# A down projection by seven block products instead of eight, on a tuned encoder layer

## The reference

```python
    up = rmsnorm(x, g_ffn) @ w_up
    a, b = up[..., :D_FF], up[..., D_FF:]
    a_ext = jnp.concatenate([conv_hist.astype(a.dtype), a], axis=1)
    conv = conv_b + sum(a_ext[:, j:j + T] * conv_w[j] for j in range(CONV_W))
    x = x + (jax.nn.silu(conv) * b) @ w_down
```

## Time and profile before

| what | value |
|---|---|
| median of 3 runs | 891.83 us (891.22 to 893.13) |
| span of the profiled execution, first to last instruction | 890.1 us |
| PE busy | 858.1 us (96%) |
| PEld busy | 825.5 us (93%) |
| DVE busy | 518.1 us (58%) |
| ACT busy | 369.1 us (41%) |
| POOL busy | 108.3 us (12%) |
| chain that ended last | PE 85%, DVE 7%, ACT 4%, DMA 2% |

### The profile page before, as it was taken

One profiled execution on the slowest core, in us unless ns is written; L12 is line 12 of the kernel. 1 busy time (PEld: TensorE's weight loads), 2 busy tenths in 40 slices (PEclk: granted clock), 3 DMA queues, 4 the chain that ended last, 5 costly groups with the idle time before them and its releaser, 6 DMA issues.

```text
span 890.1 us, 16120 instructions
## 1 busy us (share of the span) xinstructions
PE 858.1 (96%) x6155; PEld 825.5 (93%) x6155; DVE 518.1 (58%) x943; ACT 369.1 (41%) x597; POOL 108.3 (12%) x180
## 2 busy tenths in 40 slices
PE   5999999999999999999999999999999999999996
PEld 4898988998997899989999999999999999999995
DVE  2887676776664575566666566424556632455634
ACT  6576666637334454342343333212333321233324
POOL 5016475641000020000000000000000000000000
PEclk9999999999999999999999999999999999999999
DMA  6265344245237442101222233232322332232222
GB/s 209 88 207 151 113 116 111 75 144 165 79 134 267 166 142 72 48 24 56 86 87 80 74 91 94 71 94 71 94 71 71 94 86 79 72 94 76 64 73 108
DMA packets 116507, 91.22 MB, mean 102 GB/s; under 512 B 3136, under 2 KB 107798, under 8 KB 116211
## 3 DMA queue, kind: packets, MB, share of 16 engines
q1 hardware_dynamic: 111331, 73.51, 27.4%
q0 software_dynamic: 5136, 17.17, 6.4%
HBM read 81.32 MB, written 9.35 MB: 102 GB/s over the span
## 4 chain that ended last, share of the span: by engine, by line
PE 85%; DVE 7%; ACT 4%; DMA 2%; issue 2%; SPq 0%; DVEq 0%; ACTq 0%
PE ps L412 63%; PE ps L2028 4%; PE ps L2208 3%; PE ps L1921 3%; PE ps L2264 2%; PE ps L2214 1%; PE ps L2293 1%; PE ps L2314 1%; PE ps L2008 1%; DMA x_tok<-in_x_sample 1%; PE ps L2051 1%; DMA w_raw<-in_w_mk 1%; PE ps L2082 1%; PE ps L2073 1%; DVE y_tok L1882 1%
## 5 line engine op out<-in xcount | busy, mean ns | idle before, releaser
L438 DVE TENSOR_TENSOR w_lo<-w_raw,w_hi 128x1024 fp32r<-128x1024 f32 x102 | 124.9, 1224 | 170.6 <-ACT w_hi L433 168.7
L412 PE MATMUL ps<-a_hi,w_hi 128*128 128x288 f32 x896 | 193.0, 297 | 3.0 <-DVE w_lo L438 0.9
L433 ACT ACTIVATE w_hi<-w_raw 128x1024 fp32r<-128x1024 f32 x109 | 115.0, 1055 | 187.9 <-PE ps L412 179.2
L412 PE MATMUL ps<-a_hi,w_lo 128*128 128x288 f32 x896 | 191.9, 296 | 0.0
L412 PE MATMUL ps<-a_lo,w_hi 128*128 128x288 f32 x896 | 191.7, 296 | 0.0
L412 PEld LDWEIGHTS ps<-a_hi,w_hi 128*128 128x128 f32 x896 | 144.3, 189 | 4.3 <-issue 2.2
L412 PEld LDWEIGHTS ps<-a_hi,w_lo 128*128 128x128 f32 x896 | 144.3, 189 | 0.0
L412 PEld LDWEIGHTS ps<-a_lo,w_hi 128*128 128x128 f32 x896 | 144.2, 189 | 0.0
L412 PE MATMUL ps<-b_hi,w_hi 128*128 128x288 f32 x576 | 123.9, 297 | 1.0 <-DVE b_lo L445 1.0
L412 PE MATMUL ps<-b_hi,w_lo 128*128 128x288 f32 x576 | 123.4, 296 | 0.0
L412 PE MATMUL ps<-b_lo,w_hi 128*128 128x288 f32 x576 | 123.3, 296 | 0.0
(11 more groups left out here) (374 smaller groups left out, 1389.0 us busy)
## 6 DMA issues: line engine op xcount, KB each, us to landing
w_raw<-in_w_up SPq DMA_DIRECT2D x44, 512.0 KB, 3.7
w_raw<-in_w_down SPq DMA_DIRECT2D x16, 512.0 KB, 3.7
w_raw<-in_w_in SPq DMA_DIRECT2D x15, 512.0 KB, 4.1
w_raw<-in_w_o SPq DMA_DIRECT2D x8, 512.0 KB, 3.7
w_raw<-in_w_mq SPq DMA_DIRECT2D x8, 512.0 KB, 3.7
w_raw<-in_w_mo SPq DMA_DIRECT2D x8, 512.0 KB, 3.7
w_raw<-in_w_mk SPq DMA_DIRECT2D x6, 512.0 KB, 3.9
w_raw<-in_w_down SPq DMA_DIRECT2D x8, 384.0 KB, 3.4
```

The lines of the kernel that those rows point to most:

```text
L412: mm = nc.tensor.matmul(acc[:, h, 0:H], w[slot][:, c], x[:, k, h * H:h * H + H], start=(k == first and w is w_hi and x is x_hi), stop=(k = ...
L433: nc.scalar.activation(w_hi[slot][:], w_raw[slot][:], ACT.Copy).then_inc(weight_hi_ready, 1)
L438: nc.vector.tensor_tensor(w_lo[slot][:], w_raw[slot][:], w_hi[slot][:].bitcast(F32), ALU.subtract).then_inc(weight_lo_ready, 1)
```

## The change

The down projection of a chunk is computed by seven block products for each pair of output tiles, in Winograd's form of Strassen's scheme. The blocks are two output tiles (i), two neighbouring feature tiles (l) and the two token halves (j). The block sums of the weights (s1 to s4) and of the hidden tiles (`mixed`) are made on DVE, as are all low halves; ACT makes the high halves. There are 4 pairs (`DOWN_PAIRS`) of 7 products (`FACTORS`) for each chunk, and the factors are made five products ahead (`AHEAD`). A pair's seven products use three banks of PSUM; each product goes on accumulating in its bank where an earlier product of the pair was, and DVE adds or subtracts the bank to or from one block of `x_t` after each product. w_down comes as [128, nf, 256] loads of 1 MB (768 KB in the last chunk), two buffers deep. Some semaphores are merged, the transpose of the convolution's state moves from the end into the last chunk, and g_final's load and the place of `y_tok` move. The core of the diff:

```diff
+    DOWN_PAIRS = KT // 2
+    FACTORS, AHEAD = 7, 5
...
+        H00, T1, H10, H11, T2 = range(5)
+        T3, T4 = T2 + 1, T2 + 2
+        PRODUCTS = [("w00", H00, 0), ("s1", T1, 1), ("s2", T2, 0), ("w01", H10, 2),
+                    ("s3", T3, 0), ("s4", H11, 1), ("w11", T4, 0)]
+        ADDS = [(0, 0, ALU.add), (1, 1, ALU.subtract), (0, 1, ALU.add), (0, 0, ALU.add),
+                (1, 1, ALU.subtract), (0, 1, ALU.add), (1, 0, ALU.subtract)]
...
+        def down_bank(n, b):
+            return ((ps[2][:, 0], ps[2][:, 1], ps[3][:, 0]), (ps[3][:, 1], ps[1][:, 0], ps[1][:, 1]))[n % 2][b][:, 0:H]
...
SP:
-                by_columns(W_DOWN[k], a["w_down"][0, f0 * P:(f0 + nf) * P, :], k=nf)
+                for d in range(DOWN_PAIRS):
+                    n = k * DOWN_PAIRS + d
+                    if n >= 2:
+                        sp.wait_ge(down_lo_ready, FACTORS * (n - 1))
+                    rows = a["w_down"][0, f0 * P:(f0 + nf) * P, 2 * d * P:2 * (d + 1) * P]
+                    sp.dma_start(down_raw[n % 2][:, 0:nf, :], rows.rearrange(cols_k, p=P)).then_inc(down_landed[n % 2], 16)
...
POOL:
-            pool.wait_ge(acc_free, A_UP[0])
+            pool.wait_ge(weight_used, w_all)
             pool.dma_start(g_final[:], ...
ACT:
+            def down_high(g, nf):
+                n, q = divmod(g, FACTORS)
+                if q == 0:
+                    act.wait_ge(down_landed[n % 2], 16 * (n // 2 + 1))
+                if g >= AHEAD:
+                    act.wait_ge(down_done, g - AHEAD + 1)
+                if PRODUCTS[q][0] in SUM_HOME:
+                    act.wait_ge(row_sums, 4 * n + SUM_COUNT[PRODUCTS[q][0]])
+                copy(down_slot(down_hi, g, nf), down_factor(g, nf)).then_inc(down_hi_ready, 1)
...
+                if e == 0:
+                    copy(part[:, H00], hidden[0][:, 0:H]).then_inc(hidden_hi, 1)
+                    act.wait_ge(mixed_ready, m * 3 + (f0 // 2 * 3 + 1))
+                    copy(part[:, T1], mixed[:, 0]).then_inc(hidden_hi, 1)
+                else:
+                    copy(part[:, H10:H11 + 1], by_half(hidden[1][:])).then_inc(hidden_hi, 1)
+                    act.wait_ge(mixed_ready, m * 3 + (f0 // 2 * 3 + 3))
+                    copy(part[:, T2:T4 + 1], mixed[:, 1:4]).then_inc(hidden_hi, 1)
+                if last and e == 1:
+                    down_high(g0 + 4, nf)
...
DVE, a gate step (m, e), e = 0 or 1, two to a pass of the loop:
+                if last and e == 1:
+                    down_sum(g0 + 2, nf)
+                    down_low(g0 + 2, nf)
+                    down_low(g0 + 3, nf)
+                else:
+                    rest_of_weights(dve, n + 2, 0)
...             (gate, convolution, up_b and hidden as before)
+                if e == 0:
+                    minus(mixed[:, 0], x[:, 0:H], x[:, H:T]).then_inc(mixed_ready, 1)
+                    dve.wait_ge(hidden_hi, m * 4 + (2 * (f0 + e) + 1))
+                    minus(low[:, H00], x[:, 0:H], f32(high[:, H00])).then_inc(hidden_low, 1)
+                    dve.wait_ge(hidden_hi, m * 4 + (2 * (f0 + e) + 2))
+                    minus(low[:, T1], mixed[:, 0], f32(high[:, T1])).then_inc(hidden_low, 1)
+                else:
+                    nc.vector.scalar_tensor_tensor(mixed[:, 1], mixed[:, 0], -1.0, x[:, H:T], mult, sub).then_inc(mixed_ready, 1)
+                    minus(mixed[:, 2], x[:, H:T], hidden[0][:, H:T])
+                    dve.wait_ge(mixed_ready, m * 3 + (f0 // 2 * 3 + 2))
+                    nc.vector.scalar_tensor_tensor(mixed[:, 3], mixed[:, 1], -1.0, x[:, 0:H], mult, sub).then_inc(mixed_ready, 1)
+                    dve.wait_ge(hidden_hi, m * 4 + (2 * (f0 + e) + 1))
+                    minus(low[:, H10:H11 + 1], by_half(x[:]), f32(high[:, H10:H11 + 1])).then_inc(hidden_low, 1)
+                    dve.wait_ge(hidden_hi, m * 4 + (2 * (f0 + e) + 2))
+                    minus(low[:, T2:T4 + 1], mixed[:, 1:4], f32(high[:, T2:T4 + 1])).then_inc(hidden_low, 1)
+                if last and e == 1:
+                    down_sum(g0 + 4, nf)
+                    down_low(g0 + 4, nf)
+                else:
+                    rest_of_weights(dve, n + 3, 1)
+                if last and e == 0:
+                    down_low(g0, nf)
+                    down_sum(g0 + 1, nf)
+                    down_low(g0 + 1, nf)
...
DVE, after a chunk's gate steps:
+                for g in range(g0, g0 + total):
+                    more = g + AHEAD < g0 + total
+                    if more:
+                        down_sum(g + AHEAD, nf)
+                    down_add(g)
+                    if more:
+                        down_low(g + AHEAD, nf)
+                    if k + 1 < len(CHUNKS) and g - g0 in NEXT_WEIGHTS:
+                        c = NEXT_WEIGHTS.index(g - g0)
+                        rest_of_weights(dve, W_UP[k + 1] + c, c)
...
TensorE:
+            def down_product(g, nf, tiles):
+                n, q = divmod(g, FACTORS)
+                _, x, b = PRODUCTS[q]
+                first = q in (0, 1, 3)
+                for m in tiles:
+                    for w, y in ((down_hi, part_hi), (down_hi, part_lo), (down_lo, part_hi)):
+                        ins = mm(down_bank(n, b), w[g % AHEAD][:, m * P:m * P + P], y[:, m, x],
+                                 start=(first and m == 0 and w is down_hi and y is part_hi),
+                                 stop=(m == nf // 2 - 1 and w is down_lo), skip_group_check=not first)
+                if tiles[-1] == nf // 2 - 1:
+                    ins.then_inc(down_done, 1)
+
+            def down_pair(k, d):
...
+                if d == 0:
+                    pe.wait_ge(hidden_low, 2 * (f0 + nf) - 3)
...
+                pe.wait_ge(down_lo_ready, g + 1)
+                down_product(g, nf, range(half))
+                if d == 0:
+                    pe.wait_ge(hidden_low, 2 * (f0 + nf) - 2)
+                pe.wait_ge(down_lo_ready, g + 2)
+                down_product(g + 1, nf, range(half))
+                if d == 0:
+                    pe.wait_ge(down_lo_ready, g + 4)
+                    down_product(g + 3, nf, range(half - 2))
+                pe.wait_ge(down_lo_ready, g + 3)
+                pe.wait_ge(down_taken, g + 1)
+                down_product(g + 2, nf, range(half - 1))
+                if d == 0:
+                    pe.wait_ge(hidden_low, 2 * (f0 + nf))
+                down_product(g + 2, nf, range(half - 1, half))
+                pe.wait_ge(down_lo_ready, g + 4)
+                down_product(g + 3, nf, range(half - 2 if d == 0 else 0, half))
+                pe.wait_ge(down_lo_ready, g + 5)
+                pe.wait_ge(down_taken, g + 3)
+                down_product(g + 4, nf, range(half))
+                pe.wait_ge(down_lo_ready, g + 6)
+                down_product(g + 5, nf, range(half))
+                pe.wait_ge(down_lo_ready, g + 7)
+                pe.wait_ge(down_taken, g + 5)
+                down_product(g + 6, nf, range(half))
```

More of the change, by code:

```diff
@@ L302, in build @@
         silu = place("silu", [P, TE])
-        hidden = place("hidden", [P, T])
         par = place("par", [P, 6])
         conv_tok = place("conv_tok", [4 * NF, P])
+        hidden = [place(f"hidden{s}", [P, T]) for s in range(2)]
+        mixed = place("mixed", [P, 4, H])
+        down_raw = [place(f"down_raw{s}", [P, 8, 2 * P]) for s in range(2)]
+        row_sum = [place(f"row_sum{s}", [P, 4 * P]) for s in range(3)]
+        down_hi = [place(f"down_hi{s}", [P, 4 * P], F32R) for s in range(AHEAD)]
+        down_lo = [place(f"down_lo{s}", [P, 4 * P], F32R) for s in range(AHEAD)]
+        part_lo = place("part_lo", [P, 4, FACTORS, H], F32R)
+        assert here[0] <= slab_bytes
+        here[0] = at["b_hi"]
+        part_hi = place("part_hi", [P, 4, FACTORS, H], F32R)
+        assert here[0] <= at["ident"]
+        here[0] = at["a_hi"]
         y_tok = place("y_tok", [P, NT + 1, D])
@@ new lines, in down_add @@
+            def down_add(g):
+                n, q = divmod(g, FACTORS)
+                i, j, op = ADDS[q]
+                dve.wait_ge(down_done, g + 1)
+                x = x_t[:, 2 * (n % DOWN_PAIRS) + i, j * H:j * H + H]
+                nc.vector.tensor_tensor(x, x, down_bank(n, PRODUCTS[q][2]), op).then_inc(down_taken, 1)
+            for k, (f0, nf) in enumerate(CHUNKS):
+                with dve.Fori(0, nf // 2 - 1) as m:
+                    gate_step(k, m, 0)
+                    gate_step(k, m, 1)
+                gate_step(k, nf // 2 - 1, 0)
+                gate_step(k, nf // 2 - 1, 1)
+                g0, total = first_product(k), DOWN_PAIRS * FACTORS
+                for g in range(g0, g0 + total):
+                    more = g + AHEAD < g0 + total
[4 more added lines that the diff above has]
+                        down_low(g + AHEAD, nf)
+                    if k + 1 < len(CHUNKS) and g - g0 in NEXT_WEIGHTS:
+                        c = NEXT_WEIGHTS.index(g - g0)
+                        rest_of_weights(dve, W_UP[k + 1] + c, c)
```

(11 more changed lines are left out.)

263 lines of the change are left out of this document (157 added, 106 removed).

## The result

| | before | after |
|---|---|---|
| median of 4 runs each, same chip | 891.53 us (891.18 to 893.13) | 902.87 us (902.29 to 902.97) |
| ratio of times, 95% interval | | 1.0112 (1.01 to 1.0125) |
| span of the profiled execution | 890.1 us | 901.1 us |
| first matmul of the long stretch to the end of its last | 473.17 to 876.88: 403.7 us | 473.55 to 888.13: 414.6 us |

What follows compares the result with a forecast made beforehand. TensorE, in one unbroken run of matmuls at 133.4 ns each, was taken as the bound. The span was summed as 890.1 - 17.6 + 15.8 + 7.2 - 0.3 = 895.2, with 1.7 more 897 us, range 889 to 904.

Steps and rivals of the forecast that it cites:

- 132 matmuls fewer: Down projection: 924 matmuls instead of 1056, each worth 133.4 ns of TensorE time, saving 17.6 us.
- three first waits: First pair of each chunk: TensorE waits before product 2 for DVE's add of product 0; 15.8 us in all.
- (a): Rest of the pairs in the two long chunks: TensorE waits for DVE's late adds; 2.6 us together.
- (b): Last chunk's pairs: TensorE catches up with sum, ACT copy and low half twice in each pair; 3.1 us.
- (c): Second step of gate rounds: the next weights' low half comes late in eight steps; 1.5 us, bounds 0 to 4.
- clock behind the stops: Rival: after the three first waits TensorE's clock falls, costing 1.1 to 2.2 us each; 900 to 904, chance 0.25.
- the end: After the last matmul: a shorter last add and one transpose fewer ahead of it; -0.3 us.
- The waits are shorter than the saving: Rival: first waits of each chunk under 3.0 us make the kernel faster; chance 0.15, with 0.10 for a draw.
- DVE the bound of the whole stage: Rival: strided operands cost DVE what 1024 elements do, so 12 pairs lose some 50 us; 940, chance 0.05.

Runs made afterwards that it cites:

- run 9: Changed kernel with last gate round reordered, sums one product earlier, next weights first, sum for product 5 and adds of products 1 and 2 earlier; 881.42 us.
- run 2: Changed kernel with DVE's add of each chunk's first product moved right behind hidden of the last gate step; 903.37 us.
- run 5: Changed kernel with only DVE's program in the last gate round of each chunk reordered; 895.40 us.
- run 7: Changed kernel with last gate round reordered, sums one product earlier, and next weights first in every second gate step but a chunk's last; 889.24 us.
- run 1: Changed kernel with 30 extra, unused TensorE matmuls filling most of the big stop in each chunk's first pair; 899.32 us.
- run 8: Changed kernel with the four sums of w_down blocks of each pair left out, so the output differs; 888.07 us.
- run 3: Changed kernel with the four sums of w_down blocks of each pair moved from DVE to GpSimd; 893.81 us.

## Why the prediction was right, and where it was low

| term | forecast | measured |
|---|---|---|
| 132 matmuls fewer | -17.6 | -17.6 (132 x 133.4 ns; 264 of the new line take 35.30 us in run 9, 133.7 ns each) |
| three first waits | +15.8 | 5.02 + 5.21 + 4.98 = +15.2 |
| rest of the pairs, long chunks (a) | +2.6 | +1.9 + 1.75 = +3.7 |
| last chunk's pairs (b) | +3.1 | +3.1 |
| every second gate round (c) | +1.5 | +2.7 |
| clock behind the stops | 0 in the sum, a rival | +4.5 |
| the end | -0.3 | -0.3 (12.9 us from the last matmul, 13.2 before) |
| sum | +5.1 | +11.3 (the spans differ by 11.0) |

**The first waits** are right in place, cause, order and size. Runs 2, 5, 7 and 9 bear out the reason, DVE's program order, and run 9 shows that the amount of work was not the obstacle: with the same instructions TensorE keeps 12.4 of the 17.6 us (403.7 - 391.3).

**The clock** was the step that failed. The text gave the fall a chance of 0.25 and left it out of the sum, though its own row had the fall 4.7 us after the end of work and its own stop was 5.3 us long. All three stops paid, 1.3, 1.5 and 1.7 us, inside the 1.1 to 2.2 of the rival; run 1 shows that it was the clock. It is 4.5 of the 6 us by which the forecast was low; (a) and (c) are the rest, less 0.6 by which the first waits were forecast too long.

**Term (c)** was mis-sized, 2.7 for 1.5 (bounds 0 to 4). DVE is late by the 0.17 us that the working has (0.12 to 0.22) in the first chunk and by 0.3 in the others, and the slower first pair of matmuls behind any wait, 0.1 us, which the text names at the big stops, was not counted for these eight. Nor was it in **term (a)**, 3.7 for 2.6: without the slower pairs and gaps under 0.1 us its waits are 1.3 us in each long chunk, inside the 1.2 to 1.4 forecast.

**The rivals.** "The waits are shorter than the saving" fell: the add ended at 566.48, 4.9 us behind the place where product 2 was wanted. "DVE the bound of the whole stage" fell too: 128x512 low halves and sums in strided blocks take 0.69 and 0.68 us, the price of plain operands, and the later pairs of the long chunks lose only a few tenths.

What stays open: the 5.5 us of waits left in run 9 were not followed further.

## What to carry to other kernels

A cut in the busiest engine's work is worth what the helpers' program order lets through. Where a transformed product needs operands and adds in sequence, write down for every add and every factor when the busy engine asks for it, and put the helper's instructions in the order of these times: here that alone made a loss of 11 us into a gain of 11.6. Follow the second and third add too, since moving the first one only moves the wait. And where a stop of the size of an observed fall of the clock is in the forecast, the fall belongs in the sum.

## What the runs showed of the hardware

- Equal stops need not fare alike, and the clock can fall after TensorE is at work again. Run 7's two stops of 3.22 us end at 567.77 and 719.85; the windows of TensorE behind them:

```profile
568.00:569.00 1.00, 1.00 (x6) 0.53 0.85 278
...
720.00:721.00 1.00, 1.00 (x9) 1.00 0.85 260
```

The first is followed by the lower level, the second by none. The windows touch 6 matmuls and 9: the wide spacing goes with the clock and not with the length of the wait. Run 8 has the same with two stops of 2.09 us (0.50 from 566, 1.00 from 718 on). In the changed kernel the third stop's last matmul ends at 847.54 and the window from 849 already reads 0.76, so the fall came some 2 us after the end of work, where the row of before had 4.7. A stop of about 1 us (runs 1 and 9) lowered the clock nowhere, nor did run 3's waits of 1.56 and 1.46 us; the five stops of 2.27 to 2.62 us (runs 3, 5 and 7) were all followed by a fall.

- Beside a GpSimd add a DVE instruction with two SBUF operands takes up to 1.09 us longer, even one of 64 elements (0.22 to 1.31 us). In run 3 the 28 low halves of 128x512 that ran beside one took 1.3 us on average, 0.69 alone, and the 36 adds to x_t beside one 0.44 to 0.46. An idle GpSimd is no free relief for DVE.
